# Differential attention: queries and keys computed by features, rotary rows permuted on VectorE, sine product on GpSimd

## The reference

```python
qkv = h @ w_qkv                                  # h: rms_norm(x), w_qkv: 1024 x 3072
q, k, v = jnp.split(qkv, 3, axis=-1)             # 8 heads; q and k: 2 x 64 features each
q = jnp.concatenate([apply_rope(q[..., :16], cos, sin), q[..., 16:]], axis=-1)
k = jnp.concatenate([apply_rope(k[..., :16], cos, sin), k[..., 16:]], axis=-1)
# for both halves c: softmax(q_c k_c^T / 8) over whole chunks of 64 tokens
a = p[:, :, 0] - lam * p[:, :, 1]
o = rms_norm(a @ v, subln_g) * (1 - lambda_init) # then o @ w_o, added to x

def apply_rope(x, cos, sin):                     # cos, sin: 512 x 8
    x1, x2 = jnp.split(x, 2, axis=-1)
    return jnp.concatenate([x1 * c - x2 * s, x2 * c + x1 * s], axis=-1)
```

## Time and profile before

| | us |
|---|---|
| median of 3 runs | 1744.97 (1744.77 to 1745.62) |
| profiled execution | 1745.7 |
| its span in the trace | 1743.9 |
| PE busy, of the span | 1728.2 (99%) |
| DVE busy | 1091.1 (63%) |
| ACT busy | 785.4 (45%) |
| POOL busy | 134.5 (8%) |
| PE's share of the chain that ended last | 94% |
| mean granted TensorE clock | 0.998 of full speed |

### The profile page before, as it was taken

How to read it: one execution, slowest core, us unless ns; L and a number is a source line. 1 busy time by engine, 2 the same in 40 slices (tenths; PEclk the granted TensorE clock), 3 DMA queues, 4 the chain that set the end, 5 groups by cost and what they waited for, 6 DMA issues and landing times.

```text
span 1743.9 us, 22594 instructions
## 1 busy us (share of the span) xinstructions
PE 1728.2 (99%) x8782; PEld 1460.0 (84%) x8782; DVE 1091.1 (63%) x1719; ACT 785.4 (45%) x1398; POOL 134.5 (8%) x138
## 2 busy tenths in 40 slices
PE   9999999999999999999999999999999999999998
PEld 7888888888888888888888888889898888888887
DVE  5788644344346666685864764665888676376375
ACT  5553532222235555544532432456876454244244
POOL 2003200000005100002000000022101200000000
PEclk9999999999999999999999999999999999999999
DMA  5212333333333221122333333323111233333341
GB/s 169 73 51 85 93 97 97 97 97 97 97 97 97 78 69 61 61 73 85 96 97 97 97 93 101 97 76 103 39 49 37 81 92 98 98 98 97 98 127 61
DMA packets 128355, 152.78 MB, mean 88 GB/s; under 512 B 9286, under 2 KB 101992, under 8 KB 128248
## 3 DMA queue, kind: packets, MB, share of 16 engines
q1 hardware_dynamic: 128088, 151.26, 28.3%
q10 hardware_dynamic: 160, 0.07, 0.0%
HBM read 148.61 MB, written 2.10 MB: 86 GB/s over the span
## 4 chain that ended last, share of the span: by engine, by line
PE 94%; DVE 3%; ACT 1%; issue 1%; DMA 1%; POOL 0%; ACTq 0%; DVEq 0%; POOLq 0%
PE bk L1908 24%; PE bk L1909 23%; PE bk L1910 23%; PE bk L1937 5%; PE bk L1939 4%; PE bk L1938 4%; PE bk L1913 4%; PE bk L2035 2%; PE bk L2069 1%; PE bk L2068 1%; PE bk L1996 1%; PE bk L2023 1%; DVE WL L2100 1%; PE bk L2025 0%; PE bk L2024 0%
## 5 line engine op out<-in xcount | busy, mean ns | idle before, releaser
L1908 PE MATMUL bk<-R,WH 128*128 128x512 f32 x1844 | 724.0, 393 | 1.8 <-DVE R L2106 1.6
L1910 PE MATMUL bk<-R,WL 128*128 128x512 f32 x1844 | 718.4, 390 | 0.0
L1909 PE MATMUL bk<-R,WH 128*128 128x512 f32 x1844 | 718.1, 389 | 0.0
L2100 DVE TENSOR_TENSOR WL<-RAW,WH 128x1024 fp32r<-128x1024 f32 (+4 forms) x278 | 343.7, 1237 | 483.2 <-ACT WH L2302 482.2
L2302 ACT ACTIVATE WH<-RAW 128x1024 fp32r<-128x1024 f32 (+4 forms) x278 | 288.0, 1036 | 604.3 <-PE bk L1910 546.6
L1908 PEld LDWEIGHTS bk<-R,WH 128*128 128x128 f32 x1844 | 346.8, 188 | 73.4 <-issue 2.2
L1910 PEld LDWEIGHTS bk<-R,WL 128*128 128x128 f32 x1844 | 346.4, 188 | 72.8
L1909 PEld LDWEIGHTS bk<-R,WH 128*128 128x128 f32 x1844 | 346.8, 188 | 68.9
L1937 PE MATMUL bk<-WH,R 128*128 128x256 f32 (+4 forms) x432 | 146.0, 338 | 0.3 <-DVE KT L2106 0.3
L1939 PE MATMUL bk<-WL,R 128*128 128x256 f32 (+4 forms) x432 | 140.7, 326 | 0.0
L1938 PE MATMUL bk<-WH,R 128*128 128x256 f32 (+4 forms) x432 | 140.5, 325 | 0.0
(11 more groups left out here) (170 smaller groups left out, 1503.6 us busy)
## 6 DMA issues: line engine op xcount, KB each, us to landing
RAW<-in_ffn_w_up_dram SPq DMA_DIRECT2D x176, 256.0 KB, 3.0
RAW<-in_ffn_w_down_dram SPq DMA_DIRECT2D x44, 512.0 KB, 3.7
RAW<-in_w_gate_dram SPq DMA_DIRECT2D x44, 256.0 KB, 2.8
RAW<-in_w_up_dram SPq DMA_DIRECT2D x44, 256.0 KB, 3.1
RAW<-in_w_down_dram SPq DMA_DIRECT2D x22, 512.0 KB, 3.7
RAW<-in_da_w_qkv_dram SPq DMA_DIRECT2D x32, 256.0 KB, 2.9
RAW<-in_w_out_dram SPq DMA_DIRECT2D x8, 512.0 KB, 3.6
RAW<-in_da_w_qkv_dram SPq DMA_DIRECT2D x8, 512.0 KB, 3.6
```

The lines of the kernel that those rows point to most:

```text
L1908: e.matmul(dst, lh, rh, start=start, stop=False)
L1909: e.matmul(dst, lh, rl, start=False, stop=False)
L1910: return e.matmul(dst, ll, rh, start=False, stop=stop)
L2100: e.tensor_tensor(low, sides(st.n, RAW[:, r, 0:m]), high.bitcast(F32), ALU.subtract).then_inc(on["wlo_dve"], 1)
```

## The change

Queries and keys of the differential part come from `gemm_f` now. Their output has features on partitions as it leaves TensorE, 128 features (two halves of 64 of one head) by 512 tokens, four outputs m = 0 to 3 for one group (two of queries, two of keys). Per output:

- `rot_swap`: VectorE's stream_shuffle reads the bank and writes a tile in which, inside each 32 partitions, rows 0 to 7 and 8 to 15 have changed places.
- `scaled`: VectorE multiplies the bank by a table of cosines (1 for rows that aren't rotated), into another tile.
- `rot_sine`: GpSimd multiplies the permuted tile by a table of signed sines (0 for rows that aren't rotated).
- `rot_add`: VectorE adds the two.
- then the split: `hi` on ScalarE, and on VectorE `lo`, now from the tile and not from a bank; of queries with the factor 0.125.

The tables (`rot`, 128x1024, 512 KB, one load early in the program) are multiplied once by the root of the norm, which a second `over` spreads (`rotation`: four more transposes, and two `rot_spread` on VectorE). The 64 transposes of TOK, 32 `tok_qk`, 24 operations of `rope` and the small `eighth` are gone. Two rings of tiles hold the new results: 5 of sums, 3 of permuted ones. The constants lose 64 columns. Steps of the later MLA layer that use the same tiles (`tok_lat`, `mask_key`, `tok_q`) wait for more.

```diff
+        def rotation(N):
+            for x in rot.out.fr:
+                x.free = list(tok_free)
+            emit("rot_load", after=[])
+            landing(s_rot, free_at["pe"] + 20000.0)
+            while N() is None or N().rooted is None:
+                yield None
+            b = yield from bank()
+            st = yield step("over", bank=b.i, r=N().r, after=counts([b.free, N().rooted]))
+            st = yield step("rot_spread", bank=b.i, after=counts([st.pe, (s_rot, 16)]))
+            put_bank(b, st.dve)
+            rot.spread = st.dve
...
-            def ev_qk(t, bk, done):
-                free = tok_free if g < 2 else before.ups
-                while N.rooted is None or len(free) < 4:
-                    yield None
-                st = yield step("tok_qk", tok=g % 2, t=t, bank=bk.i, rq=N.r8[:, t:t + 1], rk=N.r[:, t:t + 1],
-                                after=counts([done, free, N.rooted]))
...
-                st = yield step("rope", v1=v[:, :, :, 0:8], v2=v[:, :, :, 8:16], cs=cs, sn=sn, t1=t1, t2=t2, after=counts(G.toks))
...
-                yield from turn_heads(g % 2, 0, P, n, G.cut, G.ups, q_tiles(P, G.Q))
...
-                yield from turn_heads(g % 2, 256, P, n, G.cut, G.ups, k_pair(G.kbase))
...
-            if kind == "fg":
-                yield from gemm_f(N.X, 8, 4, ev_turned)
-            else:
-                spawn(turn_in())
-                yield from gemm_t(N.X, 8, 512, ev_qk)
+            yield from gemm_f(N.X, 8, 4, ev_turned if kind == "fg" else ev_rotated)
...
+            def ev_rotated(m, bk, done):
+                while rot.spread is None or m < 2 and G.Q[m].h is None:
+                    yield None
+                z, o = (yield from taken_from(rot.swapped)), (yield from taken_from(rot.out))
+                st = yield step("rot_swap", dst=rot.at(z), bank=bk.i, after=counts([done, z.free]))
+                swapped = st.dve
+                st = yield step("scaled", dst=rot.at(o), bank=bk.i, bc=rot.cos, after=counts([done, o.free, rot.spread]))
+                turned = st.dve
+                put_bank(bk, swapped, turned)
+                st = yield step("rot_sine", z=rot.at(z), after=[swapped, rot.spread])
+                st = yield step("rot_add", z=rot.at(z), o=rot.at(o), after=[st.pool, turned])
+                rot.swapped.put(z, st.dve)
+                if m < 2:
+                    lo = yield from split_pair(G.Q[m], rot.at(o), [st.dve], 0.125)
+                else:
+                    while before and not before.valued:
+                        yield None
+                    i = G.kbase + 4 * (m - 2)
+                    lo = yield from halves(KT[:, i, :], KT[:, i + 1, :], rot.at(o), [st.dve], None, [kfree[i + x] for x in range(4)])
+                    kready[i] = [lo]
...
+                    e.tensor_tensor(rot.cos, BK[st.bank][:, :], rot.cos, ALU.mult).then_inc(on["rot_spread_dve"], 1)
+                    e.tensor_tensor(rot.sin, BK[st.bank][:, :], rot.sin, ALU.mult).then_inc(on["rot_spread_dve"], 1)
...
+                    e.stream_shuffle(st.dst, BK[st.bank][:, :], [x ^ 8 if x < 16 else x for x in range(32)]).then_inc(on["rot_swap_dve"], 1)
...
+                    e.tensor_tensor(st.o, st.o, st.z, ALU.add).then_inc(on["rot_add_dve"], 1)
...
+                    e.tensor_tensor(st.z, st.z, rot.sin, ALU.mult).then_inc(on["rot_sine_pool"], 1)
...
-                masked = yield step("mask_key", after=[])
+            masked = yield step("mask_key", after=toks)
```

More of the change, by code:

```diff
@@ L865, in put @@
                 lo = yield from split_pair(Q[n], bank[0:rows, :], [done], rows=slice(0, rows))
-                return [lo]
-            return put
-        def k_pair(base):
-            def put(n, bank, done):
-                i = base + 4 * n
-                lo = yield from halves(KT[:, i, :], KT[:, i + 1, :], bank[:, :], [done], None, [kfree[i + x] for x in range(4)])
-                kready[i] = [lo]
                 return [lo]
@@ L1211, in in_line, with taken_from @@
                 spawn(fill_by(t, pairs), 0)
+        rot = Group()
+        rot.spread, rot.cos, rot.sin = None, flat(1)[:, 0:S], flat(1)[:, S:2 * S]
+        rot.out, rot.swapped = Ring(5), Ring(3)
+        for x in rot.swapped.fr:
+            x.i += 5
+        rot.at = lambda x: flat(0)[:, x.i * S:x.i * S + S] if x.i < 5 else flat(1)[:, (x.i - 3) * S:(x.i - 2) * S]
+        def taken_from(ring):
+            while not ring.fr:
+                yield None
+            return ring.get()
+        def rotation(N):
[10 more added lines that the diff above has]
+            rot.spread = st.dve
         def qkv_group(G, g, N, kind, spent, prior=None, before=None):
@@ L1506, in ev @@
             def ev(t, bk, done):
-                while NM.rooted is None or len(Gs[2].ups) < 4:
+                while NM.rooted is None or any(len(G.ups) < 4 for G in Gs):
                     yield None
                 st = yield step("tok_lat", t=t, c0=c0, width=width, bank=bk.i, r=NM.r[:, t:t + 1],
-                                after=counts([done, Gs[2].ups, NM.rooted]))
+                                after=counts([done, [G.ups for G in Gs], NM.rooted]))
                 lat.toks.append(st.act)
@@ L1714, in da_norm @@
                 return last.n
+            last.n = None
+            spawn(rotation(lambda: last.n))
             yield from ffn(N2, value_plain, da_norm)
@@ L2348, in scalar_program @@
                     e.activation(st.dst, BK[st.bank][:, :], ACT.Copy).then_inc(on["over_copy_act"], 1)
-                elif k == "tok_qk":
-                    for done in st.after:
-                        w.wait_ge(*done)
-                    e.activation(TOKS[st.tok][:, st.t, 0:256], BK[st.bank][:, 0:256], ACT.Copy, scale=st.rq)
-                    e.activation(TOKS[st.tok][:, st.t, 256:512], BK[st.bank][:, 256:512], ACT.Copy, scale=st.rk).then_inc(on["tok_qk_act"], 1)
                 elif k == "tok_q":
@@ L2446, in gpsimd_program @@
                     e.tensor_tensor(st.v2, st.v2, st.t1, ALU.add).then_inc(on["rope_pool"], 1)
+                elif k == "rot_sine":
+                    for done in st.after:
+                        w.wait_ge(*done)
+                    e.tensor_tensor(st.z, st.z, rot.sin, ALU.mult).then_inc(on["rot_sine_pool"], 1)
                 elif k == "z_wide":
```

98 lines of the change are left out of this document (44 added, 54 removed).

## The result

| | us |
|---|---|
| before, median | 1745.1 (1744.77 to 1745.62, 4 runs) |
| after, median | 1761.41 (1760.78 to 1762.18, 4 runs) |
| ratio | 1.0091, 95% interval 1.0078 to 1.0104 |
| profiled execution of after, its span | 1760.4 |
| predicted | 1749.4, range 1741 to 1756 |

The account below looks back on a forecast made before the run. TensorE, busy 99% of the span, was taken as the bound. From the profiled 1745.7 us: -6.5 transposes, +6.6 waits for VectorE, +4.3 GpSimd meetings = 1750.1, less 0.7 to the median: 1749.4 us, range 1741 to 1756.

Parts of the forecast that it names:

- The products cost the same in either form: Query and key matmuls on TensorE: 96 of 128x512 per group before and after, swap of forms costed at 0.
- the transposes were worth 6.5: TensorE: 64 transposes of TOK go, 7.0 us; second spreading of the root adds 0.4 us; sum -6.5 us.
- the foreseen durations: VectorE: permutation, cosine product and sum taken at 0.60 us each; with two `rot_spread`, 30 us more.
- The table's load and `mask_key` cost nothing: The 512 KB table's load in the first feed-forward part and `mask_key` waiting for `tok_lat`: each costed at 0.
- Half of the meetings: Differential part: GpSimd sine products lengthen VectorE operations with tile inputs; 8.6 us if all meet, half taken, +4.3 us.
- The third rival, the lock in full: All meetings happen and slowed sine products hold sums back: 1753.7 us, or 1757.7 with a 1.1 us permutation; 18%.
- The walk: TensorE's waits for VectorE around the groups: g0 2.1, g1 0.7, g2 and g3 1.9 us each; together 6.6 us.
- The clock: Differential part: granted clock 1.00 in every window, matmuls at the upper level, so nothing to lose or win.
- Where TensorE would wait in g0: Before g1's first products near 588 us, for the low part of g1's weight chunk: 2.1 us, meetings 3.5 more.
- The first rival (the cover holds): Stalls overlap with unseen slack, no more than 2 to 3 us left of them: 1741.0 us, faster; 16%.
- the forecast without the meetings: Transposes' -6.5 us and walked waits' 6.6 us nearly cancel: 1745.0 + 0.1 = 1745.1 us, no change.

Follow-up runs that it names:

- Meetings with short GpSimd instructions: Kernel after with GpSimd's sine product cut to 8 columns, plus two 128x256 GpSimd products into a scratch tile nobody waits for: 1754.75 us.
- five banks and blocks apart: Kernel after with 5 of 8 banks for differential products, not 4, and third and fourth attention blocks of a head pair scheduled apart: 1745.94 us.
- run with the short product: Kernel after with GpSimd's sine product cut from 512 to 8 columns, order and waits unchanged: 1750.45 us.
- late settle: Kernel after with 5 banks for products, third and fourth blocks scheduled apart, and VectorE's eight settle operations at lowest rank: 1742.09 us.

## Why the prediction was right and wrong

**The ladder.** In one order and with one set of waits, that of after, VectorE's time in the part was raised step by step. All three rotation steps cut short: 1747.7 us. Permutation and sum whole: 1750.45, some 15 us of VectorE for 2.8 us of kernel. Meetings with short GpSimd instructions: 1754.75, 5.1 us for 4.3. The sine product whole on GpSimd: 1761.4, 10.7 us for 11.0. The sine product on VectorE: 1762.8, 9.6 us for 12.4. So the first 15 us of new work are mostly covered, and what comes on top counts about in full. The lowest step stands 2.6 above before, where the transposes alone would have put it 6.5 below: about 9 us are owed to that order, with the sixteen cosine products in it. The other half of the proof is the run with five banks and blocks apart: with all of the work in place and another order, 15.5 us go. The steps of the ladder are therefore prices within that order, not of the operations.

**Right.** The products cost the same in either form; the transposes were worth 6.5; VectorE's operations had the foreseen durations (permutation 0.63, cosine product 0.60, sum 0.60 where it is alone), and in the 260 us from 552 VectorE rose from 182.0 to 209.3 us. Those with a bank as an input are untouched by GpSimd, those with two tiles reach 1.5 to 1.8 us, as the earlier trace rows had shown. The rule of the Trainium skill named there (SBUF — State Buffer, "SBUF: two separate sides": an exclusive lock on a shared port pair) agrees with these rows: a lengthened 128x512 ends 0.54 us behind the GpSimd product that it met. The table's load and `mask_key` cost nothing: the same matmul starts 0.1 us later than before at 552 us, and no wait names either.

**Wrong, by the steps.**
- *Half of the meetings.* The sum took +4.3 us for GpSimd, the half of 8.6; at its 0.5 us each that is eight or nine meetings. The run with the short product is 11.0 us faster than after: there were 13 meetings of 0.8 us on an average. The prediction counted sums, low parts of queries and keys and low parts of weights. No low part of weights met a sine product. Five operations that it hadn't counted did, for 5.1 of the 10.7 us: two low parts of the heads' result and three small operations on SM. The third rival, the lock in full, was nearest, with 1753.7 and 1757.7, but for a reason that is half wrong: nothing held the sums back.
- *The walk.* The run with the short product stands 5.4 us above before, so with -6.5 from the transposes the order and VectorE's own work cost 11.9 us where the four boundaries were walked at 6.6. Measured from start to start in after, meetings included, the boundaries are 4.6 (g0), 2.7 (g1), 2.5 (g2) and 4.0 (g3), 13.8 us.
- *The clock.* "There is nothing to lose or win by it" was read from windows in which TensorE never waits. It lost 4.8 us as soon as it did. Before's own trace had a sign of it: at 1320 us, behind waits of 0.8, 0.3 and 1.0 us, its clock is low for 3.4 us.
- *Where TensorE would wait in g0.* The walk went to the low part of g1's first chunk and took it, as the text on the lists ahead of the prediction does, for the one behind the four outputs. It is the one between the `settle`: it was made at 578.05, and TensorE went on into g1's products at 588.2 without a wait. What it lacked were banks: one for the scores, to 592.15, and then, for 3.2 us, one that the low parts of g0's values had to free, which stand in VectorE's list behind two chunks of weights. The length of the list in front was right, its reader was the wrong one. That the wait expected at 2.1 to 5.6 us came, with 4.6, is luck: it came for this other reason.
- *A place not walked.* The 2.8 us near 750, at the end of g3's values, were in no term. The list of g3 differs from the others there, as no group follows, and I had walked only boundaries to a next group.
- *Not slower by more.* The first rival (the cover holds) was right about what is possible: VectorE at 84% with TensorE at 99% exists, in the kernel with late settle. It was wrong about this order.

Summed up, the forecast without the meetings was 0.1 us above before and the runs say 5.4, 5.3 too little; the meetings were priced at 4.3 and cost 11.0, 6.7 too little. Together this is 12.0, the whole distance from 1749.4 to 1761.4. The clock has no term of its own here: its 4.8 us lie in the 11.0, since the run with the short product has no low stretch in the part. How much of the 5.3 is the place at 750 is known (2.8); the rest is spread over the four boundaries and wasn't taken apart.

## What to carry to other kernels

Where one engine's list holds up TensorE, ask for every wait of TensorE which bank or part it takes, not only when weights are ready, and walk the end of the last group apart from the others. When work is given to GpSimd, count every operation of VectorE with both inputs in tiles that can stand beside it, down to those of a single column, and price each at what is left of the GpSimd instruction. Before an experiment is built to take a wait away, look in the trace whether the wait is there: the ends of the sine products and the starts of the sums were in the trace of after. And before a form is judged by its time, give the planner the freedom that it needs for it: one bank more, a finer interleaving and one rank turned a loss of 16 us to a gain of 3.4. The first two of these left the kernel before where it was; the third wasn't tried there.

## What the runs showed of the hardware

- TensorE's granted clock goes to its lower level (1.2 GHz) for 3.4 or 6.8 us right behind waits, and half of that stretch's matmul time is lost on top of the wait. It came with waits of 1.0 and 3.2 us (6.8 us low, beginning inside the second wait), of 0.8 and 0.9 us (3.4 us), and in the run without rotation one of 1.4 us (3.4 us). It isn't sure to follow: in after, the 2.6 us at 751 had no low stretch behind them, the same wait in the run with all steps cut short did (at 739.9).
- A VectorE operation with both inputs in tiles that met a GpSimd product lasted until that product was done, and its own work came after. A 128x512 ended 0.54 us behind it (582.99 to 584.44, product to 583.90). An operation of 128x1 took 1.30 us in place of 0.22, beside a product of 1.29 us.
- Each meeting was cheaper beside shorter GpSimd instructions: beside products of 128x512 (1.30 us) the lengthening was 0.3 to 1.1 us, beside two of 128x256 (0.61 us each) 0.2 to 0.5. Whether a sine product cut in two would bring its kernel anything wasn't tried.
- A stream_shuffle of 128x512 from a bank takes VectorE 0.73 us at a pace of 0.63, little more than a product of the same size, and isn't lengthened by a GpSimd operation beside it. It comes with a load of its selection (LOAD_MASK_SELECT, 13 ns) each time.
- GpSimd takes 1.30 us for a product of two 128x512 tiles, up to 2.14 where VectorE's operations with two tiles as inputs run (733.74 to 735.88); the disturbance goes both ways.
